# All heads' k first, and the triangular inverse from 32x32 blocks for all heads at once, in a decoder layer on one Trainium2 core

## Chip, cores and metric

One core of one Trainium2 chip. The metric is the device time of one launch in microseconds (us), the median of several runs. Everything is fp32. A projection multiplies in three passes of reduced fp32 (fp32r): weights and activations are each split into a high and a low part, and high by high, high by low and low by high are summed.

## What is computed

One layer (DEPTH is 1) on 512 tokens of 1024 channels, with two token mixers, a gated feed-forward part and a gated input embedding. The change touches the second mixer, the gated delta rule: 8 heads, key and value width 128, chunks of 64 tokens, so 64 chunks in all heads together. The kernel works on pairs of chunks, tiles of 128 tokens, four to a head.

```python
h = rmsnorm(x, attn_norm); proj = h @ w_in          # 1024 x 9232
qa, ka, va, qb, kb, vb, zb, bb, ab, gl = split(proj)
oa = diff_attention(rmsnorm(qa), rmsnorm(ka), va, lam, rel_bias)
qb, kb, vb = split(silu(causal_dwconv(cat(qb, kb, vb), conv_b)))
# gated_delta_rule, for each head and chunk of 64:
kkT = (k * beta) @ k.T
A = eye(64) + where(strict, kkT * decay, 0)
sol = triangular_solve(A, cat(v * beta, k * beta * exp(g)))
for chunk in chunks:                                 # carries state
    v_new = u - w @ state
    o = (q * exp(g)) @ state + (tril(q @ k.T) * decay) @ v_new
    state = state * exp(g_last) + k_dec.T @ v_new
mixed = gate0 * (oa @ w_br_a) + gate1 * (ob @ w_br_b); x = x + mixed @ w_out
# feed-forward (w_up, conv, silu gate, w_down) and embedding gate follow
```

## The kernel before, in words

The kernel is written by hand, engine by engine, with semaphores; the order on each engine is the order of the code. Weights come in chunks of 1024 x 128. For each chunk the DMA queue of SyncE (SP) loads it into one of four slots (`load`), GpSimd (in the profile POOL) makes its high part (L447) and low part (L432), and TensorE (PE) multiplies it with the normed activations (`gemm`, L493): eight steps of three matmuls of 512 columns. GpSimd takes a chunk when the chunk four before is multiplied.

`Fill.step(n)` runs the next n steps of the projection queue. TensorE's order is thus a weave: small matmuls of the attention and of the delta rule, with steps of projections between them, so that the other engines can answer in the meantime. How many steps stand where is in the tables `STEPS`, `STEPS_LEAD`, `STEPS_LATE` and `STEPS_LAST`, one for each kind of turn.

A turn (`turn`, one on each engine) takes head h's delta rule and head h + 1's attention together, and projects qb, kb, vb of head h + 1, zb of head h, and qa, ka, va of head h + 2: seven chunks, 56 steps. The first turn (`delta=False`) has attention only, the last only the delta rule. In a turn:

- Attention, for each of four blocks of queries: `scores` on TensorE (L598), `maxima` on VectorE (in the profile DVE; L1359, L1364), `softmax` on ScalarE (ACT; L960), `combine` on VectorE (L1374 to L1376), `turn_w` on TensorE (L605), `keep_w` on ScalarE; then `attend`.
- Short convolution: a first tap on ScalarE, three on VectorE (`conv`, L1390, L1394), then the silu by three ScalarE functions and a product on VectorE (`finish_silu`, L1405).
- The inverse of the unit triangular matrix of each chunk, by doubling: an inverse of blocks of size m gives that of size 2m. Six levels (n = 1 to 6), each with `ct` made by VectorE (`make_ct`, L1418), a group of matmuls (L674), a ScalarE copy (L1073), a second group (L686), a subtraction (L1488) and a 32x32-wise transpose (L1491) on VectorE. A group is eight matmuls of 64x64, two of them for each tile of 128 tokens, in the two halves of the array; in the last level four (L676, L688). For these the products k k^T (L644) are made at the start of the turn, and multiplied by the decay (L1459 to L1461), whose rows come from DRAM (`rows_of`) and are made by L1425. The norm of k enters as a scaling (`k_norm`, `start_x`, `start_wide`).
- The scan over the four tiles: `v_mm`, `vnew`, `kv`, `state` back and forth between TensorE and VectorE.

After the last turn come the gates and branches (`mix`), the output projection, the feed-forward part and the last gate. They are not touched.

## Time and profile before

| | us |
|---|---|
| median of 3 runs | 1222.64 |
| the runs | 1222.53 to 1222.65 |
| span of the profiled execution, first to last instruction | 1220.9 |
| TensorE busy | 1195.5 |
| VectorE busy | 682.4 |
| ScalarE busy | 538.4 |
| GpSimd busy | 617.8 |

No time is recorded for the profiled execution beside its span; the span is 1.7 us under the median. Busy time is the time in which an engine has an instruction under way; matmuls overlap, and the end of one is modelled, so the distance from start to start tells more than a duration. "Idle before" is the time in which the engine had nothing, in front of the instruction named, with what released it. An fp32 matmul leaves two records.

### The profile page before, as it was taken

What the parts mean: (1) busy time and instruction counts of PE and PEld (TensorE: products, weight loads), DVE (VectorE), ACT (ScalarE), POOL (GpSimd) and SP (SyncE); (2) the same over time, 40 slices, a digit from 0 to 9 for tenths busy, and PEclk for the clock granted to TensorE, in tenths of its full rate; (3) what the DMA queues carried; (4) which work ended last, traced back from release to release, by engine and by line L of the source; (5) the groups of instructions that cost most, each with busy time, mean ns of one, the idle gap of its engine ahead of it and who ended that gap; (6) DMA issues with size and microseconds to landing.
All of it is one profiled execution on the core that took longest, in us unless ns stands there. A gap on an engine that the chain in (4) does not pass through costs nothing.

```text
span 1220.9 us, 19031 instructions
## 1 busy us (share of the span) xinstructions
PE 1195.5 (98%) x6526; PEld 931.7 (76%) x6526; DVE 682.4 (56%) x1157; ACT 538.4 (44%) x923; POOL 617.8 (51%) x766
## 2 busy tenths in 40 slices
PE   6999999999999999999999999999999999999998
PEld 4766777777776777776777888888888888888886
DVE  5267576767768576767221323456677713651634
ACT  4364645455454636454232222354444423432542
POOL 5553443544453432635545645456656664573552
PEclk9999999999999999999999999999999999999999
DMA  8313130313121211312222342233333342232223
GB/s 261 91 43 99 27 93 18 99 33 95 35 78 53 62 35 43 106 52 69 70 70 77 105 163 86 87 99 107 98 93 103 89 118 85 87 111 78 71 80 90
DMA packets 192404, 102.66 MB, mean 84 GB/s; under 512 B 3798, under 2 KB 191177, under 8 KB 192329
## 3 DMA queue, kind: packets, MB, share of 16 engines
q1 hardware_dynamic: 191948, 101.55, 29.3%
q8 instruction: 42, 0.69, 0.2%
q14 instruction: 33, 0.27, 0.1%
q10 hardware_dynamic: 381, 0.15, 0.0%
HBM read 99.57 MB, written 2.13 MB: 83 GB/s over the span
## 4 chain that ended last, share of the span: by engine, by line
PE 90%; DVE 6%; ACT 3%; issue 1%; DMA 1%; ACTq 0%; DVEq 0%
PE bank L493 74%; PE bank L686 2%; PE bank L674 2%; PE bank L598 2%; PE bank L612 1%; PE bank L568 1%; DVE dec L1425 1%; PE bank L605 1%; DVE oa_lo L1585 1%; PE bank L644 1%; PE bank L723 1%; PE bank L627 1%; PE bank L653 1%; PE bank L731 1%; DMA slope<-bias_line 0%
## 5 line engine op out<-in xcount | busy, mean ns | idle before, releaser
L432 POOL TENSOR_TENSOR w_lo<-w_raw,w_hi 128x256 fp32r<-128x256 f32 x692 | 544.4, 819 | 261.2 <-ACT w_hi L877 255.5
L493 PE MATMUL bank<-hn_hi,w_hi 128*128 128x512 f32 x1000 | 423.8, 424 | 1.0 <-DVE o_a L1592 1.0
L493 PE MATMUL bank<-hn_hi,w_lo 128*128 128x512 f32 x1000 | 391.6, 392 | 0.0
L493 PE MATMUL bank<-hn_lo,w_hi 128*128 128x512 f32 x1000 | 391.2, 391 | 0.0
L447 POOL CAST w_hi<-w_raw 128x1024 fp32r<-128x1024 f32 x70 | 73.7, 1052 | 325.4 <-PE bank L493 296.9
L493 PEld LDWEIGHTS bank<-hn_hi,w_hi 128*128 128x128 f32 x1000 | 188.3, 188 | 48.6 <-issue 11.6
L493 PEld LDWEIGHTS bank<-hn_hi,w_lo 128*128 128x128 f32 x1000 | 187.8, 188 | 41.1
L493 PEld LDWEIGHTS bank<-hn_lo,w_hi 128*128 128x128 f32 x1000 | 188.6, 189 | 36.5 <-issue 6.5
L877 ACT ACTIVATE w_hi<-w_raw 128x1024 fp32r<-128x1024 f32 x111 | 117.9, 1062 | 75.8 <-PE bank L493 68.2
L1692 DVE SCALAR_TENSOR_TENSOR u<-vr,pt,u 128x511 f32<-128x511 f32 x88 | 88.8, 1009 | 8.0 <-DVE u L1692 0.2
L1686 DVE TENSOR_TENSOR vr<-bank,rs 128x512 f32<-128x512 f32 x44 | 30.4, 692 | 73.3 <-PE bank L493 67.8
L493 PE MATMUL bank<-fa_hi,w_hi 128*128 128x512 f32 x176 | 68.5, 389 | 0.0
L493 PE MATMUL bank<-fa_hi,w_lo 128*128 128x512 f32 x176 | 68.5, 389 | 0.0
L493 PE MATMUL bank<-fa_lo,w_hi 128*128 128x512 f32 x176 | 68.5, 389 | 0.0
L1211 ACT ACTIVATE u<-vr,pt 128x512 f32<-128x512 f32 x44 | 35.9, 816 | 38.9 <-DVEq L1687 38.2
L1073 ACT ACTIVATE ui<-bank 128x256 f32<-128x256 f32 (+1 forms) x48 | 18.4, 383 | 64.9 <-PE bank L674 58.7
L966 ACT ACTIVATE wT<-bank 128x128 f32<-128x128 f32 (+3 forms) x32 | 14.0, 438 | 72.0 <-PE bank L605 72.0
L1726 DVE TENSOR_TENSOR x<-x,bank 128x512 f32 x16 | 11.0, 688 | 61.3 <-PE bank L493 60.6
L1216 ACT ACTIVATE fa_hi<-tn 128x512 fp32r<-128x512 f32 x22 | 13.9, 633 | 65.6 <-DVE tn L1704 65.6
L960 ACT ACTIVATE pr<-bank,ast 128x128 f32<-128x128 f32 (+3 forms) x64 | 33.8, 528 | 18.7 <-DVE ast L1364 16.8
L1629 DVE TENSOR_TENSOR sg<-sg,bank 128x512 f32<-128x512 f32 x8 | 5.5, 688 | 62.9 <-PE bank L493 62.9
L1488 DVE TENSOR_TENSOR xi<-xi,bank 128x256 f32<-128x256 f32 x40 | 16.9, 421 | 41.9 <-PE bank L686 40.7
(277 smaller groups left out, 1770.4 us busy)
## 6 DMA issues: line engine op xcount, KB each, us to landing
w_raw<-in_w_in SPq DMA_DIRECT2D x73, 512.0 KB, 5.0
w_raw<-in_w_up SPq DMA_DIRECT2D x44, 512.0 KB, 3.8
w_raw<-in_w_down SPq DMA_DIRECT2D x16, 512.0 KB, 4.2
w_raw<-in_w_br_a SPq DMA_DIRECT2D x8, 512.0 KB, 4.2
w_raw<-in_w_br_b SPq DMA_DIRECT2D x8, 512.0 KB, 4.2
w_raw<-in_w_out SPq DMA_DIRECT2D x8, 512.0 KB, 4.2
w_raw<-in_w_ple_gate SPq DMA_DIRECT2D x8, 512.0 KB, 4.2
w_raw<-in_w_down SPq DMA_DIRECT2D x8, 384.0 KB, 3.5
```

Source lines behind the costliest of these rows:

```text
L432: ins = pool.tensor_tensor(wlo[c.slot][:, ks, :], raw[c.slot][:, ks, :], whi[c.slot][:, ks, :].bitcast(F32), ALU.subtract)
L447: pool.tensor_copy(whi[c.slot][:, :, :], raw[c.slot][:, :, :]).then_inc(high_ready, 1)
L493: mm = pe.matmul(acc, w[c.slot][:, i, :], xx[:, x0 + i, :], start=(i == 0 and n == 0), stop=last)
L598: mm = pe.matmul(bank[3 + j][:, 0:(i + 1) * P], qa[s, i * P:(i + 1) * P], ka[s, 0:(i + 1) * P], start=True, stop=True)
L674: mm = pe.matmul(packed(7, 0, t, q), ct[n % 2][q, t, :], xi[q, t, :], start=True, stop=True)
L686: mm = pe.matmul(packed(5, 0, t, q), xt[q, t, :], ui[q, t, :], start=True, stop=True)
L877: done(nc.scalar.activation(whi[c.slot][:, :, :], raw[c.slot][:, :, :], ACT.Copy), high_ready, c.number + 1)
L960: done(nc.scalar.activation(pr[j][:, 0:w], bank[3 + j][:, 0:w], ACT.Exp, bias=ast[:, 2 + j:3 + j], scale=-1.0, accum_out=ast[:, 4 + j:5 + j]),
L1073: done(nc.scalar.activation(ui[q, :, :], packed(7, part=q), ACT.Copy), "ui", h * (NL - 1) + n)
L1211: done(nc.scalar.activation(u[:, :], v[:, :], ACT.Identity, bias=col(PA_FBIAS + q * KF, f), scale=col(PA_TAP[2] + q * KF, f)), "u_made", 2 ...
L1686: done(V.tensor_tensor(v[:, :], bank[c.bank][:, :], rs[:, :], ALU.mult), bank_free[c.bank], c.uses + 1)
L1692: link(V.scalar_tensor_tensor(out=u[:, back:], in0=v[:, 0:T - back], scalar=col(PA_TAP[j] + q * KF, f), in1=u[:, back:], op0=ALU.mult, op1 ...
```

## The change

- The k projections of all eight heads are multiplied first (`stream.keys`), with their convolution, silu, products k k^T (`key_products`) and decay (`key_decay`, `lower`). The turns have six chunks, 48 steps; the first has five and a function of its own, `lead_turn`. k stays in `o_b`, whose place is free until each head's result is written.
- The level loop goes. `gather` transposes the four diagonal strips of 32 rows, so that each of the 128 partitions holds one 32x32 block: 32 tiles of 128 tokens, four blocks each. `substitute` then solves all 128 blocks at once by forward substitution, 31 steps of a product and a subtraction on VectorE over (31 - j)(j + 1) columns. It is cut into seven pieces that stand between head 0's attention pieces. `scatter` transposes the result into `xf`, which now lies in the free part of `o_a` for all heads and is zeroed by GpSimd at the start.
- The last two levels, 32 to 64 and the pair term that the second chunk of a tile needs, are made for all heads in `pair_low`, `pair_high` (32 matmuls of 32x32 each, two groups of each) and `half_low`, `half_high` (eight matmuls of 64x64 each, four groups of each), with ScalarE copies between them and VectorE taking the result (`pair_take`, `half_take`).
- The norms of k are read from the diagonal of the k products in one piece (`key_norms`).
- New step tables, and on ScalarE and VectorE another order inside the turn: the q silu comes before block 2's softmax, vb's silu before block 3's weights are kept.

```diff
--- before.py
+++ after.py
...
-LEVELS = (1, 2, 4, 8, 16, 32, 64)
-NL = len(LEVELS)
-STEPS = ((3, 2, 1, 1, 2), (2,) * 6, (1, 1, 1, 1, 1, 1), (3, (1, 1), (1, 1, 1), (1, 1, 1), (1, 1, 1)), (3, 6))
-STEPS_LEAD = (4, (5, 1, 1, 1, 2), (2, 1, 3, 2, 2, 2), (2, 0, 2, 0, 2, 0), (2, (1, 1), (1, 1), (1, 1), (1, 1)), (0, 1))
-STEPS_LATE = ((3, 2, 1, 1, 2), (2,) * 6, (1, 1, 1, 1, 1, 1), (3, (1, 0), (1, 1, 1), (1, 1, 1), (1, 1, 1)), (0, 0))
-STEPS_LAST = ((7, 2, 2, 3, 3), (3,) * 6, (4, 3, 3, 3, 3, 3), (3, (1, 1), (1, 1, 2), (1, 2, 2), (1, 2, 2)), (0, 0))
+SUB = 32
+ROWS = 4 * H
+STEPS = ((2, 3, 2, 3, 3, 1, 3, 3, 1, 5), ((1, 1), (1, 1, 1), (1, 1, 1), (1, 1, 1)), (3, 3))
+STEPS_LATE = ((3, 3, 1, 3, 3, 1, 2, 2, 1, 3), ((1, 0), (1, 1, 1), (1, 1, 1), (1, 1, 1)), (0, 0))
+STEPS_LAST = ((2, 3, 2, 3, 4, 1, 3, 3, 1, 3), ((1, 1), (2, 2, 2), (2, 2, 2), (2, 2, 2)), (0, 0))
...
+FIRST = ("qa", "ka", "va")
+TURN = ("qb", "vb", "zb", "qa", "ka", "va")
+LEAD = ("qb", "vb", "qa", "ka", "va")
+LATE = ("qb", "vb", "zb", "zl")
+KEY_BANKS = (5, 6, 7)
...
+            key_rows(0)
+            key_rows(1)
+            for n in range(5, H):
+                load(stream.keys.at(n), w_in0, COLS["kb"] + n * P)
+                key_rows(n - 3)
+            for n, name in enumerate(FIRST):
+                load(stream.first.at(n), w_in0, COLS[name])
+                key_rows(n + 5)
+            for n, name in enumerate(LEAD):
+                load(stream.lead.at(n), w_in0, COLS[name] + (AHEAD[name] - 1) * P)
+                if n == 0:
+                    rows_of(0)
...
+            f = Fill(*[gemm(stream.keys.at(n), hn_hi, hn_lo) for n in range(H)],
+                     *[gemm(stream.first.at(n), hn_hi, hn_lo) for n in range(len(FIRST))])
+            f.step(2)
...
+            def key_products(h):
+                b = KEY_BANKS[h % 3]
+                pe.wait_ge(sem("k_silu"), h + 1)
+                if h == 0:
+                    pe.wait_ge(sem("cum_turned"), 1)
+                elif h < 3:
+                    pe.wait_ge(sem("bias_ready"), H // 2)
+                else:
+                    pe.wait_ge(sem("lower"), h - 2)
+                for t in range(NT):
+                    s = slice(t * P, (t + 1) * P)
+                    mm = pe.matmul(tiles(b)[:, t, :], key(h)[:, s], key(h)[:, s], start=True, stop=True)
+                mm.then_inc(sem("kk"), 1)
...
+            for h in range(H):
+                f.step(2)
+                key_products(h)
+                f.step(6)
...
+            def pair_low(g):
+                b = (5, 7)[g]
+                pe.wait_ge(sem("blocks"), 1)
+                for n in range(HALF):
+                    m = g * HALF + n
+                    at = slice(n * SUB, (n + 1) * SUB)
+                    pe.matmul(bank[b][strip(1), at], dd[strip(0), m, SUB:2 * SUB], xf[strip(0), m, HEAD:HEAD + SUB],
+                              start=True, stop=True)
+                    mm = pe.matmul(bank[b][strip(3), at], dd[strip(2), m, SUB:2 * SUB], xf[strip(2), m, 3 * SUB:P],
+                                   start=True, stop=True)
+                mm.then_inc(sem("inverse_u"), 1)
...
+            def half_low(g):
+                b = (5, 7)[g % 2]
+                pe.wait_ge(sem("pairs"), 1 if g == 0 else 2)
+                if g > 1:
+                    pe.wait_ge(sem("xf_ready"), g - 1)
+                for n in range(8):
+                    m = g * 8 + n
+                    mm = pe.matmul(bank[b][UP, n * HEAD:(n + 1) * HEAD], lt6[LOW, m, :], xf[LOW, m, UP],
+                                   start=True, stop=True)
+                mm.then_inc(sem("inverse_u"), 1)
...
+            def lead_turn(at, fill):
+                f = Fill(*fill)
+                scores(0, 0)
+                f.step(8)
+                turn_w(0, 0)
+                f.step(2)
+                scores(0, 1)
+                f.step(8)
+                turn_w(0, 1)
+                f.step(2)
+                scores(0, 2)
+                f.step(6)
+                turn_w(0, 2)
+                f.step(2)
+                scores(0, 3)
+                f.step(4)
+                k_turn(0)
+                pair_low(0)
+                pair_low(1)
+                f.step(2)
+                turn_w(0, 3)
+                v_turn(0)
+                pair_high(0)
+                pair_high(1)
+                f.step(2)
+                attend(0)
+                half_low(0)
+                qk_sum(1, 0, at("qa"))
+                half_low(1)
+                f.step(1)
+                attention_sum(0)
+                half_high(0)
+                half_high(1)
+                f.step(1)
+                half_low(2)
+                qk_sum(1, 1, at("ka"))
+                half_low(3)
+                f.step(1)
+                half_high(2)
+                half_high(3)
+                f.rest()
...
-                for n in range(1, NL):
-                    if delta:
-                        if n < NL - 1:
-                            pe.wait_ge(sem("ct"), h * (NL - 1) + (n + 1))
-                        pe.wait_ge(sem("xi"), h * (NL - 1) + n)
-                        for t in range(NT):
-                            if n < NL - 1:
-                                for q in (LOW, UP):
-                                    mm = pe.matmul(packed(7, 0, t, q), ct[n % 2][q, t, :], xi[q, t, :], start=True, stop=True)
-                            else:
-                                mm = pe.matmul(packed(7, 0, t, UP), lt6[:, t, :], xi[LOW, t, :], start=True, stop=True)
-                        mm.then_inc(sem("level_u"), 1)
-                    f.step(first[n - 1])
-                    if delta:
-                        pe.wait_ge(sem("ui"), h * (NL - 1) + n)
-                        pe.wait_ge(sem("xt"), h * NL + n)
-                        if n == 1 and h > 0:
-                            pe.wait_ge(sem("ob_sum_read"), h)
-                        for t in range(NT if n < NL - 1 else 0):
-                            for q in (LOW, UP):
-                                mm = pe.matmul(packed(5, 0, t, q), xt[q, t, :], ui[q, t, :], start=True, stop=True)
-                        for t in range(NT if n == NL - 1 else 0):
-                            mm = pe.matmul(packed(5, 1, t, LOW), ui[UP, t, :], xt[UP, t, :], start=True, stop=True)
-                        mm.then_inc(sem("level_vt"), 1)
...
+                f.step(before[6])
+                if attention:
+                    k_turn(a)
+                f.step(before[7])
+                if attention:
+                    turn_w(a, 2)
+                f.step(before[8])
+                if attention:
+                    scores(a, 3)
+                pe.wait_ge(sem("xf_ready"), H // 2)
+                pe.wait_ge(sem("turned_read"), h + 1)
+                pe.matmul(tiles(7)[:, 0, :], xf[:, h * NT, :], vbt[:, 0, :], start=True, stop=True).then_inc(sem("v_mm"), 1)
+                f.step(before[9])
...
+            def lower(h):
+                b, d, m = KEY_BANKS[h % 3], decs[h % 2], slice(h * NT, (h + 1) * NT)
+                dve.wait_ge(sem("kk"), h + 1)
+                dve.wait_ge(sem("key_dec"), h + 1)
+                V.tensor_tensor(lt6[LOW, m, :], tiles(b)[LOW, :, UP], d[LOW, :, UP], ALU.mult)
+                V.tensor_tensor(dd[LOW, m, :], tiles(b)[LOW, :, LOW], d[LOW, :, LOW], ALU.mult)
+                done(V.tensor_tensor(dd[UP, m, :], tiles(b)[UP, :, UP], d[UP, :, UP], ALU.mult), "lower", h + 1)
...
+            def gather():
+                for b in range(4):
+                    at = SUB * (b % 2)
+                    ins = V.transpose(li[strip(b), :, :], dd[strip(b), :, at:at + SUB].rearrange("p n i -> p i n"))
+                link(ins)
+                done(V.transpose(ksum[:, :], wide(li)[:, 0:SUB * SUB:SUB + 1]), "k_sums", 1)
+                link(V.memset(xs[:, :, :], 0.0))
...
+            def substitute(j0, j1):
+                for j in range(j0, j1):
+                    n, w = SUB - 1 - j, j + 1
+                    part = prod[:, 0:n * w].rearrange("p (i c) -> p i c", c=w)
+                    link(V.tensor_tensor(part, li[:, w:SUB, j:w].to_broadcast([P, n, w]),
+                                         xs[:, j:w, 0:w].to_broadcast([P, n, w]), ALU.mult))
+                    link(V.tensor_tensor(xs[:, w:SUB, 0:w], xs[:, w:SUB, 0:w], part, ALU.subtract))
...
+            def scatter():
+                dve.wait_ge(sem("xf_zero"), 1)
+                place_rows(0, HEAD)
+                place_rows(2, 3 * SUB)
+                place_columns(1)
+                done(place_columns(3), "blocks", 1)
...
+            def lead_turn(at):
+                substitute(0, 6)
+                prep(0, 0)
+                prep(0, 1)
+                substitute(6, 11)
+                maxima(0, 0)
+                substitute(11, 15)
+                combine(0, 0)
+                steps(conv(0, 0, at("qb")))
+                maxima(0, 1)
+                substitute(15, 20)
+                combine(0, 1)
+                steps(finish_silu(0, 0))
+                substitute(20, 23)
+                maxima(0, 2)
+                substitute(23, 26)
+                steps(conv(0, 2, at("vb")))
+                combine(0, 2)
+                substitute(26, 31)
+                maxima(0, 3)
+                scatter()
+                combine(0, 3)
+                scatter_rest()
...
+            for h in range(H):
+                steps(conv(h, 1, stream.keys.at(h)))
+                if h == 0:
+                    for n in range(H // 2):
+                        bias_copy(n)
+                if h > 1:
+                    lower(h - 2)
+                if h > 0:
+                    key_decay(h - 1)
+                steps(finish_silu(h, 1))
+            lower(H - 2)
+            key_decay(H - 1)
+            lower(H - 1)
+            gather()
+            scale_rows()
...
```

TensorE, in a turn of before, from the scores of block 2 on: one level group (L674), two steps, the second group (L686). The names after the arrow are the inputs, the numbers the output's size.

```order
L598 MATMUL bank<-ka,qa 128x384 x2
L674 MATMUL bank<-xi,ct 64x64 x8
L493 MATMUL bank<-hn_hi,w_hi 128x512
L493 MATMUL bank<-hn_lo,w_hi 128x512
L493 MATMUL bank<-hn_hi,w_lo 128x512
...
L686 MATMUL bank<-ui,xt 64x64 x8
```

Twelve such groups stood in each turn, each in front of its steps.

TensorE now, in `lead_turn`, after a step of projection (L524): k's transposes (L676 in the new file), then the 32x32 groups (L696, L698; 64 such rows for both `pair_low`).

```order
L524 MATMUL bank<-hn_lo,w_hi 128x512
L524 MATMUL bank<-hn_hi,w_lo 128x512
L676 MATMUL bank<-sq,o_b 128x128 x4
L696 MATMUL bank<-o_a,dd 32x32
L698 MATMUL bank<-o_a,dd 32x32
```

The level groups have left the turns, and all heads' small matmuls follow each other here without steps between them.
VectorE, in a turn of before: level operations between the attention's and the convolution's.

```order
L1418 TENSOR_TENSOR ct<-lt,sq 128x256
L1488 TENSOR_TENSOR xi<-xi,bank 128x256
L1491 STREAM_TRANSPOSE xt<-xi 128x256
L1390 SCALAR_TENSOR_TENSOR kb<-bank,pt,kb 128x511
L1390 SCALAR_TENSOR_TENSOR kb<-bank,pt,kb 128x510
L1394 SCALAR_TENSOR_TENSOR kb<-bank,pt,kb 128x509
L1359 TENSOR_TENSOR bank<-bank,bias 128x256 x2
L1364 TENSOR_REDUCE ast<-bank 128x1 x2
L1488 TENSOR_TENSOR xi<-xi,bank 128x256
```

These level operations leave VectorE's turns.

VectorE now, ahead of head 0's attention: gather, the norms, the row scaling and the first steps of the substitution (L1637, L1639; 62 such rows, up to 256 columns).

```order
L1618 STREAM_TRANSPOSE li<-dd 32x1024 x4
L1620 STREAM_TRANSPOSE ksum<-li 128x32
L1621 MEMSET xs 128x1024
L1626 TENSOR_TENSOR kz<-kz,gates 128x32
L1628 STREAM_TRANSPOSE kzb<-kz 128x32
L1629 COPY xs<-kzb 128x32
L1630 TENSOR_TENSOR li<-li,kzb 128x1024
L1637 TENSOR_TENSOR prod<-li,xs 128x31
L1639 TENSOR_TENSOR xs<-xs,prod 128x31
L1637 TENSOR_TENSOR prod<-li,xs 128x60
L1639 TENSOR_TENSOR xs<-xs,prod 128x30x2
```

They stand in front of everything of the lead; `prep(0, 0)`, for which TensorE's `scores(0, 0)` waits, follows six of the steps.
TensorE, in a turn of before, the last rows between the scores of block 3 and its turned weights (L605); ahead of these rows stand seven more steps and three level groups.

```order
L493 MATMUL bank<-hn_hi,w_lo 128x512
L688 MATMUL bank<-xt,ui 64x64 x4
L493 MATMUL bank<-hn_hi,w_hi 128x512
L493 MATMUL bank<-hn_lo,w_hi 128x512
L493 MATMUL bank<-hn_hi,w_lo 128x512
L622 MATMUL bank<-sq,kb 128x128 x4
L708 MATMUL bank<-vbt,xf 128x128
...
L493 MATMUL bank<-hn_hi,w_lo 128x512
L605 MATMUL bank<-sq,pr 128x128 x4
L586 MATMUL bank<-sq,va_raw 128x128 x4
```

The two level groups, and more of them further up, stood between scores and weights.

TensorE now, from those scores (L650 here) to the turned weights (L657): one small matmul (L829) and five steps, of which the middle is left out.

```order
L650 MATMUL bank<-ka,qa 128x512 x2
L829 MATMUL bank<-vbt,o_a 128x128
L524 MATMUL bank<-hn_hi,w_hi 128x512
L524 MATMUL bank<-hn_lo,w_hi 128x512
L524 MATMUL bank<-hn_hi,w_lo 128x512
...
L524 MATMUL bank<-hn_hi,w_lo 128x512
L657 MATMUL bank<-sq,pr 128x128 x4
L638 MATMUL bank<-sq,va_raw 128x128 x4
```

Of what stood between the two, k's transposes and the level groups are gone, the first to an earlier place.

## Rows read from the trace of the kernel before

**Rows 1.** The page's first lines: span, and one engine's busy time, share and instructions.

```profile
span 1220.9 us, 19031 instructions
PE 1195.5 (98%) x6526; PEld 931.7 (76%) x6526; DVE 682.4 (56%) x1157; ACT 538.4 (44%) x923; POOL 617.8 (51%) x766
```

**Rows 2.** Busy us in stretches: PE, weight load, VectorE, ScalarE, GpSimd, then granted clock, DMA.

```profile
51.00:97.00 46.00, 42.42 (x184) 29.62 (x182) 29.19 (x56) 27.65 (x61) 22.82 (x27) 1.00 0.35 91
163.00:229.00 66.00, 65.40 (x445) 47.75 (x444) 46.84 (x93) 34.70 (x75) 28.25 (x36) 1.00 0.22 58
```

**Rows 3.** TensorE by line, shapes apart, one of the level loop's groups: busy us, mean ns, idle before.

```profile
L674 PE MATMUL bank<-xi,ct 64*64 64x64 f32 x640 | 27.2, 224 | 0.0
```

**Rows 4.** TensorE in order of time, one level group between projection matmuls.

```profile
238.58 0.39 PE L493 MATMUL bank<-hn_hi,w_lo 128*128 128x512 f32 x1
238.90 0.68 PE L674 MATMUL bank<-xi,ct 64*64 64x64 f32 x16
239.51 0.50 PE L493 MATMUL bank<-hn_hi,w_hi 128*128 128x512 f32 x1
...
240.08 0.40 PE L493 MATMUL bank<-hn_hi,w_lo 128*128 128x512 f32 x1
```

**Rows 5.** VectorE's groups by line, shapes apart.

```profile
L1418 DVE TENSOR_TENSOR ct<-lt,sq 128x256 f32<-128x256 f32 x40 | 24.4, 610 | 2.2 <-DVE qb L1394 1.1
L1425 DVE SCALAR_TENSOR_TENSOR dec<-crow,gates,sq 128x128 f32<-128x128 f32 x32 | 14.5, 515 | 0.4 <-DVE vb L1394 0.2
L1390 DVE SCALAR_TENSOR_TENSOR kb<-bank,pt,kb 128x511 f32<-128x511 f32 x8 | 6.0, 750 | 0.3
L1491 DVE STREAM_TRANSPOSE xt<-xi 128x256 f32<-128x256 f32 x32 | 14.3, 445 | 1.1
L1493 DVE STREAM_TRANSPOSE xt<-xi 32x128 f32<-32x128 f32 x8 | 2.4, 300 | 0.3
```

**Rows 6.** VectorE in order of time: two runs of one operation, and a small one.

```profile
92.85 0.17 DVE L1433 TENSOR_TENSOR kz<-kz,gates 128x4 f32<-128x4 f32 x1
...
246.48 0.43 DVE L1418 TENSOR_TENSOR ct<-lt,sq 128x256 f32<-128x256 f32 x1 [0.16 <-DVE qb L1394]
250.56 0.84 DVE L1418 TENSOR_TENSOR ct<-lt,sq 128x256 f32<-128x256 f32 x1
```

**Rows 7.** All engines in order of time, from a block's scores to its turned weights.

```profile
73.17 1.13 PE L598 MATMUL bank<-ka,qa 64*128 64x512 f32 x4
...
74.44 0.77 DVE L1359 TENSOR_TENSOR bank<-bank,bias 128x256 f32<-128x256 f32 x2 [0.16 <-PE bank L598]
75.23 1.29 DVE L1364 TENSOR_REDUCE ast<-bank 128x1 f32<-128x512 f32 x2
...
77.42 0.69 ACT L960 ACTIVATE pr<-bank,ast 128x512 f32<-128x512 f32 x1
...
79.55 1.11 DVE L1376 SCALAR_TENSOR_TENSOR pr<-pr,ast 128x512 f32<-128x512 f32 x1
...
80.71 0.66 PE L605 MATMUL bank<-sq,pr 128*128 128x128 f32 x4 [0.27 <-DVE pr L1376]
```

**Rows 8.** TensorE in order of time, the same two places in a turn.

```profile
190.34 1.13 PE L598 MATMUL bank<-ka,qa 64*128 64x512 f32 x4
...
201.49 0.60 PE L605 MATMUL bank<-sq,pr 128*128 128x128 f32 x4
```

**Rows 9.** Order of time at the start, TensorE and then GpSimd.

```profile
8.80 3.19 PE L537 MATMUL bank<-sq,x_tok 128*128 128x128 f32 x12 [8.80 <-DVE x_tok L1290]
...
18.80 0.78 PE L493 MATMUL bank<-hn_hi,w_hi 128*128 128x512 f32 x1
19.37 0.58 PE L493 MATMUL bank<-hn_lo,w_hi 128*128 128x512 f32 x1
19.78 0.40 PE L493 MATMUL bank<-hn_hi,w_lo 128*128 128x512 f32 x1
...
12.69 1.04 POOL L447 CAST w_hi<-w_raw 128x1024 fp32r<-128x1024 f32 x1 [12.23 <-DMA w_raw<-in_w_in]
```

778 lines of the change are left out of this document (405 added, 373 removed).

## The prediction

> **What bounds the kernel now.** I read the shares of busy time first, then the stretches, then TensorE's groups and its order of time. TensorE is busy 98% of the span [rows 1]. In the stretches the reader is to see that this holds from head to head: in a turn of 66 us (the work from one `scores(a, 0)` to the next) TensorE lacks 0.6 us, VectorE is busy 47 and ScalarE 35; only between 51 and 97 us, where the first head has attention and no delta rule, are 3.6 us missing [rows 2]. So time goes only where TensorE's own work goes, and it comes back wherever TensorE must wait. The change takes work from TensorE and gives VectorE a long serial chain. The sum has therefore two parts: TensorE's work, and TensorE's waits.
>
> I sum against the profiled execution, whose span is 1220.9 us. The median of the runs is 1222.64, so 1.7 us lie around the span, and I add them at the end. A measurement of this kernel tells about 0.2%, 2.4 us, from no change.
>
> **TensorE's work, removed.** Per head there are six levels of two groups of small matmuls, 96 groups in all (the 640 records of [rows 3] are the first groups of five levels; each fp32 matmul leaves two). What one costs is read from the order of time, not from the 0.68 us that it is drawn with: projection matmuls follow each other by 0.23 us, but from the one that starts at 238.58 to the third after the group at 240.08 there are 1.50 us where three steps would take 0.69 [rows 4]. So a group costs 0.81 us, and 96 cost 77.8 us. The k projections (eight steps of 0.69 us each) and the k products move from the turns to the front; they are no saving.
>
> **TensorE's work, added.** Four groups of 32 matmuls with 32 columns (`pair_low`, `pair_high`), and eight groups of eight 64x64 matmuls on one half of the array (`half_low`, `half_high`). For the latter the nearest row is the level group itself, eight matmuls of 64x64 of which two halves run side by side: of its 0.81 us I take 0.43 as four in a row (0.107 each: 64 columns, four passes, at 2.4 GHz) and 0.38 as the change-over; eight in a row make 0.86 + 0.38 = 1.24 us, and eight groups 9.9 us. No row shows 32 columns. At the columns' pace (half of 0.107 a matmul, two strips side by side) a pair group takes 0.85 us; at the pace of L674's records (0.61 us for 16 [rows 4], 64 records here) 2.4. I take 1.7, in the middle; four make 6.8 (3.4 to 9.8). Together 16.7. So TensorE's work falls by 77.8 - 16.7 = **61.1 us**.
>
> The Trainium skill gives this one price directly: TensorEngine Tiling (Array Packing), "Instruction Overhead", says that a matmul of one column takes as long as one of 60. By it a 32-column matmul costs no less than a 64-column one, and the pair groups would stand near the upper end, 3 us more than I take. No run here shows it yet.
>
> **Waits in front.** From about 25 us TensorE runs the eight k projections, then qa, ka, va of head 0, with the k products two steps into the projection after next. Per head VectorE has there three taps (3 x 0.75), the decay rows (14.5 us for eight heads, 1.8 each), three products with the decay and the silu product (512 columns each in all, 1.3 and 0.75), near 6.2 us [rows 5]; TensorE has 5.5 and 0.95 for the k product. They balance; I count 1 us of waits, and 0.7 at the bias matmuls, whose copies now stand behind a convolution. After the last k silu VectorE alone carries the chain up to `blocks`, for which `pair_low` waits:
> - lower for two heads and one decay: 4.3
> - eight 32x32 transposes of 1024 columns, four to gather and four to scatter. 128 columns take 0.30 and 256 take 0.445 us [rows 5], so 1024 take about 1.3: 10.5 (lower bound as computed; if the far strides double it, 21)
> - the zeroing of xs, row scaling and three small ScalarE steps for the norms: 4.3
> - the substitution: 31 steps of two linked operations. The columns of a step are (31-j)(j+1), 5456 in the sum. 4 columns take 0.17 and 256 take 0.43 us when undisturbed, so 0.165 us + 1.04 ns a column, and 0.04 from link to link: 62 x 0.205 + 2 x 5456 x 0.00104 = 24.1. But the same 256 columns take 0.61 in the mean and 0.84 at worst, in TENSOR_TENSOR from SBUF, when GpSimd is at work [rows 5, 6]. I take 26, a quarter of the operations disturbed; the ends are 24 and 43
> - prep 1.6, head 0's maxima (6.5, by widths from the 0.77 + 1.29 of block 3 in [rows 7]), three combines (3.9), two convolutions and a silu (5.3): 17.3
> - tap and scores to wait for after each resumption of TensorE: 2.5.
>
> Sum 65 us. TensorE has over the same stretch 46 steps of 0.69, 31.7, and 7.5 of k product, scores, turns and sums: 39.2. So it waits **26 us**, in five pieces of 4 to 7 us before `scores(0, 0)`, three `turn_w` and `pair_low`. After `blocks` the rounds TensorE, ScalarE, VectorE of the two lower levels hide behind attend and the sums of squares, but for 1 us. The waits of before in this part go: 3.6 us by [rows 2] and 0.3 ahead of them. Net 1 + 0.7 + 26 + 1 - 3.9 = **+24.8 us**.
>
> **Waits in the turns.** A turn shrinks from 66 to 49.8 us of TensorE's work: eight steps (5.5), a k product (0.95) and twelve level groups (9.7) are gone. Those groups had been cover for the softmax. The chain from the scores of block 3 to its turned weights is, in an undisturbed place, VectorE from 74.44, ScalarE's two exponentials to 78.2, VectorE to 80.66, TensorE at 80.71; the scores ended at 74.3, so 6.1 to 6.4 us [rows 7]. In a turn of before, 10 us of other work lay between the two [rows 8]; the order now has one small matmul and five steps, 3.75 us. So TensorE must wait 2.4 us each turn. By the same rows block 2 has 5.8 us of chain (ScalarE takes the q silu ahead of the softmax) behind 4.75 us of cover, wait 1.0; and the sum of squares of ka, for which ScalarE must first finish qa's root, waits 0.7. With the chain's lower end that is 4.0 us in each of six turns, 24; the late turn has three steps and two steps fewer of cover there, 6.5; the last turn's wait for ob_scaled 1.2. VectorE and ScalarE themselves are not full, some 34 and 27 of 53 us. The 5 us of waits that the seven turns have now (0.6 each by [rows 2]) are replaced. Net **+26.7 us**.
>
> **Costed at nothing.** GpSimd's zeroing of xf, 4096 columns, 4 us by its CAST of 1024 in 1.05, is hidden ahead of its first cast, which waits for data until 12.69 us [rows 9]; uncovered it would be 4 us. The k loads stand in SP's queue behind `cum_turned` and behind the rows of the decay two heads back; each gets there 10 us or more before its multiplication. If the decays came late, the loads of qa, ka, va would be next. GpSimd splits seven projections in 28 us of a turn now [rows 2], so six take 24 of 50.
>
> **Sum.** 1220.9 - 61.1 + 24.8 + 26.7 = 1211.3; with the 1.7 us around it **1213 us**, 0.8% faster. In place: head 0's delta turn starts near 183 us instead of 97, and from there on everything is 96 us shorter.
>
> **Rivals.**
> 1. *The covers suffice* (chance 0.2). I chain single durations; if waits overlap more than I see, the turns lose 10 instead of 32 us and the front 20. Then 1213 - 22 - 6 = 1185; half of it gives 1199. For it: the order keeps five steps in reserve at each turn's end. Against it: [rows 7].
> 2. *VectorE's chain in front is longer, and the change loses* (0.17). Place: substitution, gather, scatter; mechanism: contention with GpSimd, which splits weights meanwhile, and strides of 128 or 256 bytes in the transposes. At their upper ends they add 15 and 10 us, each in full to TensorE's wait: 1213 + 25 = 1238; from 7 us on it is no gain beyond the measurement, from 12 us on a loss. Half of it gives about 1226, and I price it at 1231. For it: 0.84 against 0.43. Against it: GpSimd itself runs dry while TensorE waits.
> 3. *TensorE's clock falls in the waits* (0.1). At its start, after 8.8 us without work, it works 10 us on transposes, and then the first projection matmuls are still 0.57 and 0.41 apart, and 0.23 later [rows 4, 9]; the page's granted clock reads full (2.4 GHz) in this stretch all the same, so only the spacing tells. If each of five waits brings this back for as much work as there, 5 us each, of which the later waits hide the half: +13, 1226. The waits of under 1 us in the turns [rows 2] did no such thing; 4 to 7 us are not shown. The Trainium skill, TensorE: Matmul & The Clock Gate, "HAM oscillation", warns of just this: idle gaps send the clock to 1.2 GHz and each burst starts cold. By it this rival would be the rule and not the exception; the small waits of this trace neither bear it out nor refute it.
> 4. *The levels were no cost*, because other work took their place (0.03): 1240 or more. The order of time in rows 4 speaks against it.
>
> **How the numbers follow.** My forecast has 0.5, at 1213, with its own range of 1204 to 1222. The range of 1195 to 1231 leaves out the far halves of rivals 1 and 2. Faster by over 0.2% (under 1220.2): nearly nine tenths of the forecast, all of rival 1 and a fifth of rival 2 and 3 together: 0.69. Within 0.2%: 0.12. Slower: most of rival 2, rival 4 and some of 3: 0.19.
>
> **What would show it.** TensorE's busy time near 1134 us, and its idle time before `scores(0, 0)`, the `turn_w` of head 0 and the first 32x32 group in pieces of 4 to 7 us; turns of 53 to 54 us, with waits of 2 to 3 us before the four transposes of `turn_w(a, 3)`, put down to VectorE's pr; the substitution's operations at 0.2 to 0.45 us. Head 0's delta turn starts near 183 us. I am wrong if a turn takes under 51 or over 56 us, if the substitution takes over 35 us, or if projection matmuls after a wait follow by more than 0.23 us for long.

## The result, and the profile after

| | before | changed |
|---|---|---|
| median, us | 1222.59 | 1240.51 |
| the runs, us | 1222.46 to 1222.65 | 1238.85 to 1241.61 |
| span of the profiled execution, us | 1220.9 | 1239.8 (own time 1241.6) |
| TensorE busy, us | 1195.5 | 1153.6 |

The change makes the kernel slower by 1.4%: ratio 1.0144, 95% interval 1.013 to 1.0159, against 1213 forecast and outside its range. Against the 1211.3 us forecast for the span of the profiled execution, 28.5 us are missing.

The page's first lines, its clock row and its shares of the chain, to be read beside [rows 1]:

```profile
span 1239.8 us, 16629 instructions
PE 1153.6 (93%) x5502; PEld 909.3 (73%) x5502; DVE 662.9 (53%) x1061; ACT 509.2 (41%) x798; POOL 620.3 (50%) x767
PEclk9997879999999999999999999999999999999999
PE 75%; DVE 16%; ACT 5%; issue 3%; ACTq 0%; DVEq 0%
```

TensorE's busy time fell by 41.9 us where 61.1 were forecast, and its idle time rose from 25.4 to 86.2 us, by 60.8 where 51.5 were forecast. The clock row has a dent that the one before did not have. The stretches (the columns of [rows 2]) say where; the first five are the lead, the work from the last k to head 0's delta turn, then come two full turns:

```profile
97.00:113.00 16.00, 3.98 (x17) 2.68 (x17) 15.03 (x24) 2.70 (x6) 10.73 (x14) 0.70 0.37 98
113.00:137.00 24.00, 17.34 (x63) 12.66 (x61) 20.81 (x44) 5.01 (x13) 8.28 (x10) 0.85 0.00 1
137.00:151.00 14.00, 8.53 (x30) 5.83 (x30) 12.05 (x24) 4.34 (x10) 3.96 (x5) 0.88 0.00 0
151.00:166.00 15.00, 7.88 (x29) 5.33 (x29) 12.70 (x19) 3.44 (x8) 0.00 (x0) 0.73 0.00 1
166.00:196.00 30.00, 29.11 (x430) 22.73 (x430) 19.46 (x25) 14.73 (x24) 4.64 (x6) 0.85 0.37 90
252.00:308.00 56.00, 51.34 (x244) 37.27 (x242) 31.49 (x61) 27.24 (x53) 25.20 (x30) 1.00 0.24 62
308.00:365.00 57.00, 52.38 (x243) 38.32 (x242) 31.48 (x61) 27.24 (x53) 25.19 (x30) 0.97 0.23 61
```

The mean granted clock of the lead is 0.70 to 0.88 of full speed: it goes to and fro between its two levels, 2.4 and 1.2 GHz. Of the two turns the second lasts 1.6 us longer, at 0.97. TensorE in order of time shows its waits in the lead and in one turn (from the block-0 scores at 308.00 to the next at 364.92):

```profile
112.67 0.80 PE L650 MATMUL bank<-ka,qa 64*128 64x128 f32 x4 [12.02 <-DVE ka L1515]
123.71 0.47 PE L657 MATMUL bank<-sq,pr 128*128 128x128 f32 x1 [2.92 <-DVE pr L1542]
137.20 0.56 PE L657 MATMUL bank<-sq,pr 128*128 128x128 f32 x2 [3.94 <-DVE pr L1542]
151.19 0.90 PE L657 MATMUL bank<-sq,pr 128*128 128x128 f32 x3 [5.46 <-DVE pr L1542]
166.26 0.26 PE L696 MATMUL bank<-o_a,dd 32*32 32x32 f32 x1 [7.20 <-DVE o_a L1646]
...
321.40 0.44 PE L657 MATMUL bank<-sq,pr 128*128 128x128 f32 x2 [0.57 <-DVE pr L1542]
329.26 0.55 PE L657 MATMUL bank<-sq,pr 128*128 128x128 f32 x3 [1.08 <-DVE pr L1542]
337.70 0.66 PE L657 MATMUL bank<-sq,pr 128*128 128x128 f32 x4 [2.26 <-DVE pr L1542]
338.19 0.60 PE L638 MATMUL bank<-sq,va_raw 128*128 128x128 f32 x4
338.55 0.58 PE L524 MATMUL bank<-hn_hi,w_hi 128*128 128x512 f32 x1
338.93 0.63 PE L524 MATMUL bank<-hn_lo,w_hi 128*128 128x512 f32 x1
339.36 0.63 PE L524 MATMUL bank<-hn_hi,w_lo 128*128 128x512 f32 x1
...
360.41 1.13 PE L625 MATMUL bank<-sqr,sq 128*128 128x512 f32 x2 [0.71 <-ACT sqr L1043]
```

The five waits of the lead are there, 31.5 us in all (26 forecast), at the places named, though of 2.9 to 12.0 us and not of 4 to 7; the turns' waits too, 4.6 us a turn (4.0 forecast), the one before block 1's `turn_w` not foreseen. And behind the wait of 2.26 us the projection matmuls are 0.43 us apart, not 0.23: the slow clock. VectorE's groups in the lead, shapes apart, answer to [rows 5]:

```profile
L1618 DVE STREAM_TRANSPOSE li<-dd 32x1024 f32<-32x1024 f32 x4 | 8.0, 2002 | 0.1
L1646 DVE STREAM_TRANSPOSE o_a<-xs 32x1024 f32<-32x1024 f32 x4 | 7.7, 1927 | 0.1
L1642 DVE STREAM_TRANSPOSE o_a<-xs 32x1024 f32<-32x1024 f32 x3 | 6.6, 2191 | 0.1
```

A transpose of 1024 columns takes 2.0 us, not 1.3. From the last k silu (88.1) to `blocks` (166.2) VectorE's chain takes 78.1 us where I had 65, and VectorE is without work for 6.2 of them.

From these rows two theories. **Theory 1:** the clock is what is missing; it makes TensorE's work in the lead longer, and the 13 us by which head 0's delta turn is late (196.1 instead of 183) are the clock's. **Theory 2:** VectorE's chain sets the end of the lead at any clock, and the turns lack cover; the clock costs only where TensorE itself is the bound. The runs that follow were judged against the kernel before on the same chip (1222.4 to 1222.8 us); differences below are to the 1240.5 of the changed kernel, whose runs spread by about 1.4 us each way.

### The profile page after: what moved, and what is told of

Its sections match the earlier page's. It is cut to its first block, busy times and chain, and to the rows that moved or that the text cites. A ratio compares the mean times of both kernels' runs of the same rounds, so it can differ in the third digit from the quotient of the medians.

```text
span 1239.8 us, 16629 instructions
## 1 busy us (share of the span) xinstructions
PE 1153.6 (93%) x5502; PEld 909.3 (73%) x5502; DVE 662.9 (53%) x1061; ACT 509.2 (41%) x798; POOL 620.3 (50%) x767
## 4 chain that ended last, share of the span: by engine, by line
PE 75%; DVE 16%; ACT 5%; issue 3%; ACTq 0%; DVEq 0%
PE bank L524 64%; DVE pr L1542 2%; PE bank L664 1%; DVE pr L1541 1%; PE bank L625 1%; ACT pr L1077 1%; DVE dec L1587 1%; DVE o_b L1556 1%; DVE qb L1556 1%; DVE xs L1639 1%; PE bank L650 1%; DVE vb L1556 1%; DVE prod L1637 1%; PE bank L657 1%; DVE ast L1530 1%
## 5 line engine op out<-in xcount | busy, mean ns | idle before, releaser
L524 PE MATMUL bank<-hn_hi,w_hi 128*128 128x512 f32 x1000 | 421.7, 422 | 1.0 <-DVE o_a L1815 1.0
L524 PE MATMUL bank<-hn_hi,w_lo 128*128 128x512 f32 x1000 | 395.4, 395 | 0.0
L524 PE MATMUL bank<-hn_lo,w_hi 128*128 128x512 f32 x1000 | 394.9, 395 | 0.0
L524 PEld LDWEIGHTS bank<-hn_hi,w_hi 128*128 128x128 f32 x1000 | 191.0, 191 | 49.0 <-issue 15.2
L524 PEld LDWEIGHTS bank<-hn_hi,w_lo 128*128 128x128 f32 x1000 | 190.7, 191 | 42.1
L524 PEld LDWEIGHTS bank<-hn_lo,w_hi 128*128 128x128 f32 x1000 | 191.3, 191 | 38.2 <-issue 5.7
L524 PE MATMUL bank<-fa_hi,w_hi 128*128 128x512 f32 x176 | 68.5, 389 | 0.0
L524 PE MATMUL bank<-fa_lo,w_hi 128*128 128x512 f32 x176 | 68.5, 389 | 0.0
L524 PE MATMUL bank<-fa_hi,w_lo 128*128 128x512 f32 x176 | 68.5, 389 | 0.0
L657 PE MATMUL bank<-sq,pr 128*128 128x128 f32 x80 | 16.8, 312 | 42.2 <-DVE pr L1542 42.2
L657 PEld LDWEIGHTS bank<-sq,pr 128*128 128x128 f32 x80 | 9.4, 150 | 54.2 <-DVE pr L1542 53.9
L650 PE MATMUL bank<-ka,qa 64*128 64x128 f32 (+3 forms) x128 | 27.4, 506 | 12.8 <-DVE ka L1515 12.8
```

Source lines behind the costliest of these rows:

```text
L524: mm = pe.matmul(acc, w[c.slot][:, i, :], xx[:, x0 + i, :], start=(i == 0 and n == 0), stop=last)
L650: mm = pe.matmul(bank[3 + j][:, 0:(i + 1) * P], qa[s, i * P:(i + 1) * P], ka[s, 0:(i + 1) * P], start=True, stop=True)
L657: mm = pe.transpose(bank[3][:, t * P:(t + 1) * P], pr[0][:, t * P:(t + 1) * P], ident)
```

## Experiments

**The clock alone, in the lead.**

```diff
+W = (48, 18, 22, 28, 34)
...
+            def warm(n):
+
+                for _ in range(n):
+                    pe.matmul(bank[5][:, :], hn_hi[:, 0, 0:P], hn_hi[:, 0, :], start=True, stop=True)
...
+                pe.wait_ge(sem("lower"), H)
+                warm(W[0])
                 scores(0, 0)
                 f.step(8)
+                warm(W[1])
                 turn_w(0, 0)
...
```

> The changed kernel, with 150 single-pass matmuls of 512 columns into a free bank placed in the five waits before scores(0, 0), turn_w(0, 0) to turn_w(0, 2) and pair_low (48, 18, 22, 28, 34 of them, 0.23 us each at full clock); they compute nothing that is used and fit into the waits. Theory 1 (the clock did it: TensorE's busy time is 1153.6 us where 1134 was forecast, and the clock is the whole reason why head 0's delta turn starts 13 us late): the granted clock stays at 2.4 GHz from 97 to 196 us, scores(1, 0) start near 183 instead of 196.1, and the time falls by 13 us to about 1227. Theory 2 (VectorE's chain up to `blocks` sets the end of the lead, at whatever clock TensorE runs): the clock is full too, but pair_low starts at 162 to 165 instead of 166.3, only the 3 to 4 us in which VectorE waited for slow TensorE work and the 4 us of slow work behind 166 come back: 1232 to 1236. If the slow clock cost nothing: 1240.

Measured: 1234.2 us (1233.5 to 1236.1), 6.3 less. Two stretches of the lead, and TensorE at the start of head 0's delta turn:

```profile
97.00:113.00 16.00, 14.93 (x66) 11.62 (x65) 14.94 (x27) 2.70 (x6) 10.08 (x12) 1.00 0.31 84
151.00:166.00 15.00, 15.00 (x102) 11.38 (x102) 13.51 (x19) 3.00 (x7) 0.00 (x0) 1.00 0.00 1
```

```profile
191.77 0.49 PE L651 MATMUL bank<-ka,qa 64*128 64x128 f32 x4 [0.74 <-DVE ka L1527]
```

In the lead the clock was full but for one short piece near 125 us (0.93 between 113 and 137), behind the one longer wait that was left, of 1.9 us. Yet `pair_low` started at 165.4, only 0.8 earlier than without: up to there VectorE's chain sets the pace. From there to `scores(1, 0)` it took 26.3 us instead of 29.9, so the clock costs about 4 us in the lead (0.8 and 3.5), not 13. Theory 2. (The rest of the 6.3 came with two slow pieces of the late turn that this run happened not to have.)

**The chain without the substitution, and the longest wait moved.**

```diff
             def substitute(j0, j1):
 
-                for j in range(j0, j1):
+                for j in ():
```

> The 31 steps of the substitution are left out, so what follows computes with inverse blocks that hold the diagonal alone. They take 28.7 us of VectorE from start to start. Theory 2 (VectorE's chain): nearly all of it comes out of TensorE's waits before pair_low (31.5 us in all), the remaining waits are near 5 us, the clock's drops in the lead go with them: 25 to 33 us less, 1207 to 1215. Theory 1 (the clock alone is what is missing, VectorE's chain is covered by something else): 13 us less at most, 1227.

```diff
-                substitute(0, 6)
-                prep(0, 0)
-                prep(0, 1)
-                substitute(6, 11)
+                substitute(0, 11)
                 maxima(0, 0)
...
             gather()
+            prep(0, 0)
+            prep(0, 1)
             scale_rows()
```

> Only VectorE's order changes: the two operations that make qa and ka of head 0 stand behind the gather and not behind the first six steps of the substitution. The longest single wait of TensorE, 12.0 us before scores(0, 0), must shrink to about 4. Theory 2 (what counts is the length of VectorE's chain up to `blocks`, and it is the same): the later waits grow by as much, pair_low starts at 162 to 166 us, and only part of VectorE's 6 us of idle time between its pieces and of the slow clock goes: 1236 to 1240. Rival (the wait before scores(0, 0) is itself the loss): 8 us less, 1232.

Without the substitution 1218.7 us, 21.8 less; the first 32x32 group started at 146.9 instead of 166.3. That is beyond theory 1 (13 at most), and short of the 25 to 33 I expected: between 113 and 137 us VectorE was then busy for 12.9 us only. Attention's own round between the three engines had probably become the chain; no run tests that by itself. With the order changed 1239.9 us, 0.7 less, within the spread: `scores(0, 0)` at 106.3 instead of 112.7, but 8.4 us of wait before the next `turn_w` instead of 2.9, and `pair_low` at 165.4. A single wait is not a loss by itself; the chain's length is.

**Why a transpose takes 2.0 us.**

```diff
-                place_rows(0, HEAD)
-                place_rows(2, 3 * SUB)
-                place_columns(1)
-                done(place_columns(3), "blocks", 1)
+                for b in range(4):
+                    ins = V.transpose(xf[strip(b), 8 * b:8 * b + 8, :], xs[strip(b), :, :])
+                done(ins, "blocks", 1)
```

> The four 32x32 transposes before `blocks` (2.05 us each) are given contiguous operands of the same size, so their blocks land in wrong places of xf. If strides are what makes 1024 columns cost 2.0 us, each takes 1.3 to 1.4 us (a 512-column one of o_a takes 0.70) and the time falls by 2.6 us to 1238. If it is the size, or GpSimd, they stay at 2.0 and the time at 1240.5.

Measured: 1235.7 us, 4.8 less (2.6 expected), more than the 3.3 us of the transposes. They took 1.24 us each; the gather, left with its stride of 256 bytes, 2.0 as before:

```profile
L1618 DVE STREAM_TRANSPOSE li<-dd 32x1024 f32<-32x1024 f32 x4 | 8.0, 2011 | 0.1
L1652 DVE STREAM_TRANSPOSE o_a<-xs 32x1024 f32<-32x1024 f32 x4 | 4.9, 1236 | 0.1
```

So it is the stride, and it costs 0.8 us per 1024 columns. The Trainium skill, SBUF — State Buffer, has a note on "SBUF cachelines": accesses in a row that each go to another 16-byte line pay a penalty. The trace agrees in direction; the size, 60%, is this run's. Of the 1.5 us that the transposes don't account for, 0.9 are there already when the gather begins (93.7 instead of 94.7), before anything that the edit touches: they are the spread from run to run.

**Cover in the turns.**

```diff
-STEPS = ((2, 3, 2, 3, 3, 1, 3, 3, 1, 5), ((1, 1), (1, 1, 1), (1, 1, 1), (1, 1, 1)), (3, 3))
+STEPS = ((2, 3, 2, 3, 4, 1, 3, 4, 1, 8), ((1, 0), (1, 1, 1), (1, 1, 1), (1, 1, 1)), (0, 3))
```

> Only the table of fill steps of the six full turns changes: block 3's softmax gets 8 steps of cover instead of 5, blocks 1 and 2 one step more each, taken from the three steps before the sum of squares of qa, from one behind t = 0 of the scan and from the reserve at the turn's end. If too little cover makes the waits (0.57 + 1.08 + 2.27 + 0.70 = 4.6 us a turn): the first three go to 0 to 0.3 each, the last grows to at most 2, turns take 52 to 53 us instead of 55.3, and the turns in which the clock dropped (56.6 and 56.9) take no more than the others: 1217 to 1224. If the waits only move (to the scan, to the sums or to scores(a, 0)): turns stay at 55 and the time is 1236 to 1241.

Measured: 1215.7 us (1214.4 to 1216.8), 24.8 less, and 0.6% under the kernel before (ratio 0.9942, 0.9928 to 0.9955). Turns are 52.44 us apart (the first 51.8). One of them:

```profile
320.47 0.55 PE L657 MATMUL bank<-sq,pr 128*128 128x128 f32 x3 [0.54 <-DVE pr L1542]
329.22 0.66 PE L657 MATMUL bank<-sq,pr 128*128 128x128 f32 x4 [0.56 <-DVE pr L1542]
347.71 1.13 PE L625 MATMUL bank<-sqr,sq 128*128 128x512 f32 x2 [0.72 <-ACT sqr L1043]
```

That is a little beyond the 1217 expected at best. Nothing moved elsewhere: the wait for the sum of squares stayed at 0.7, none appeared in the scan. No turn had the slow clock. The six turns won 22.4 us, of which 4.6 by the clock (the run below).

**The clock alone, in the turns.**

`idle(n)` issues the same matmuls as `warm(n)` above; the late turn is the one with `more_a` false.

```diff
                 if attention:
+                    if not more_a:
+                        pe.wait_ge(sem("ob_sum_read"), h)
+                        idle(8)
                     turn_w(a, 2)
...
                 if attention:
+                    if h > 0:
+                        pe.wait_ge(sem("ob_sum_read"), h)
+                    idle(8 if more_a else 10)
                     turn_w(a, 3)
```

> The changed kernel with idle matmuls only in the waits of the turns: 8 before each turn_w(a, 3) (1.8 of 2.27 us), in the late turn 8 and 10 before turn_w(7, 2) and turn_w(7, 3). The waits' ends and the order are as they were. If the slow clock in turns (turns 0, 2 and 5 took 56.6 to 56.9 us, the others 55.3; two drops in the late turn) comes from these waits: all six turns take 55.3 to 55.5 us and the time falls by 6 to 8 us: 1232 to 1235. If the drops come from elsewhere in a turn: three turns of 56.9 remain, 1240.

Measured: 1233.6 us (1232.7 to 1234.4), 6.9 less. All turns take 55.4 us (the first 55.0), the stretch of the six has full clock, and so has what follows:

```profile
196.00:528.00 332.00, 314.64 (x1491) 230.60 (x1489) 187.97 (x365) 161.81 (x316) 150.72 (x181) 1.00 0.24 63
```

The drops do come from these waits. In the changed kernel a wait of 2.1 to 2.3 us, the only longer one in a turn, brought the slow clock in three turns of six, at 1.6 us each; no drop in the turns of any run stands behind one of the waits of 0.5 to 1.1 us. In between lies one of 1.9 us in the lead, behind which the clock fell in e1 and not in e13 below.

**What a level group had cost.**

```diff
+                    self.f, self.h, self.left = f, h, 12 if h < H - 2 else 0
...
+                        self.f.step()
+                        if self.left:
+                            self.left -= 1
+                            for t in range(NT):
+                                for q in (LOW, UP):
+                                    pe.matmul(bank[7][q, t * HEAD:(t + 1) * HEAD], key(self.h)[q, 0:HEAD],
+                                              key(self.h)[q, t * P:t * P + HEAD], start=True, stop=True)
```

> The changed kernel with twelve groups of eight 64x64 matmuls put back into each of the six full turns, on idle data into a free bank, one behind each of the first twelve fill steps (the work that the change took out, without its waits). At 0.81 us a group, as forecast, a turn takes 55.3 - 0.6 + 9.7 = 64.4 us; at 0.68, the time a group is drawn with, 62.9. Whichever it is, 12 groups a turn must cost more than the 8.9 us that turns actually lost of TensorE's work, if the last level's two groups of four matmuls were cheaper than the rest: 64.4 says so, 63.6 says that all groups cost 0.74. The waits before turn_w(a, 2) and turn_w(a, 3) remain.

Measured: 1288.8 us, and 64.87 us a turn. Of these 3.4 are waits (0.42, 2.27 and 0.70; block 1's is covered) and 1.6 the clock, which fell in every turn. So the work is 59.9 us, 9.2 more than the changed kernel's 50.7: 0.77 a group. Alone between steps a group costs 0.81 as in [rows 4], right ahead of other small matmuls 0.61:

```profile
323.45 0.40 PE L524 MATMUL bank<-hn_hi,w_lo 128*128 128x512 f32 x1
323.78 0.68 PE L793 MATMUL bank<-o_b 64*64 64x64 f32 x16
...
324.96 0.40 PE L524 MATMUL bank<-hn_hi,w_lo 128*128 128x512 f32 x1
325.28 0.68 PE L793 MATMUL bank<-o_b 64*64 64x64 f32 x16
325.89 1.16 PE L815 MATMUL bank<-qb,o_b 128*128 128x128 f32 x8
```

A turn of the kernel before took 66.6 us (228.46 to 295.09) with 0.6 of waits; less eight steps, a k product and the 50.7 that remain, its twelve groups were worth 8.9 us, not my 9.7. What I expected of this run, that the last level's two groups of four matmuls had been the cheaper ones, the trace of the kernel before refutes:

```profile
328.07 0.39 PE L493 MATMUL bank<-hn_hi,w_lo 128*128 128x512 f32 x1
328.39 0.68 PE L676 MATMUL bank<-xi,lt 64*64 64x64 f32 x8
...
329.58 0.40 PE L493 MATMUL bank<-hn_hi,w_lo 128*128 128x512 f32 x1
```

From the matmul before the group to the third behind it are 1.51 us, as the 1.50 of [rows 4]: four matmuls on one half of the array cost the same 0.81 as eight on two halves side by side. What was cheaper are the groups next to other small matmuls, three of twelve in a turn of before and four of twelve here. With these at 0.61 the twelve come to 9.1 and 8.9 us (9 x 0.81 + 3 x 0.61, 8 x 0.81 + 4 x 0.61), within 0.3 of what was measured, 8.9 and 9.2.

**A shorter gather, which first made it slower.** ScalarE lays out the diagonal blocks of each head (`compact(h)`), so that one transpose of 128 partitions replaces four.

```diff
+                for b in range(4):
+                    at = SUB * (b % 2)
+                    ins = nc.scalar.activation(xs[strip(b), :, m], dd[strip(b), m, at:at + SUB].rearrange("p n i -> p i n"), ACT.Copy)
+                done(ins, "compacted", h + 1)
...
                 if h > 0:
                     key_decay_exp(h - 1)
+                if h > 1:
+                    compact(h - 2)
...
-                for b in range(4):
-                    at = SUB * (b % 2)
-                    ins = V.transpose(li[strip(b), :, :], dd[strip(b), :, at:at + SUB].rearrange("p n i -> p i n"))
-                link(ins)
+                dve.wait_ge(sem("compacted"), H)
+                link(V.transpose(li[:, :, :], xs[:, :, :]))
```

> The gather as one transpose of 128 partitions with contiguous operands: ScalarE copies the diagonal blocks of each head, as lower makes them, into a tile that is laid out for it (four copies of 128 columns a head, in the phase of the keys where it is half idle). Chain before: four transposes, 8.05 us. Now 1.3 us for one (1.24 us was the contiguous one of the run e3_flat_tr), and some 1.2 us for the last head's copies. Theory 2: 5 to 6 us come out of the chain and of the time: 1234 to 1236. If a transpose over 128 partitions costs four times one over 32, or ScalarE's copies hold up the silus of the keys: no gain, 1240 or more.

> The steps of e4_steps, the gather of e6_compact, and qa and ka of head 0 behind three steps of the substitution instead of six. If the effects add: 1215.7 less 5 to 7, 1209 to 1211. If the shorter chain is eaten by more time at half clock: 1213 or more.

> The same with idle matmuls in the five waits of the lead (8, 14, 18, 24, 24 of them, 0.23 us each). e1_warm_lead won 6.3 us, of which some 4 in the lead and 2 in the late turns. If the clock's price stands beside the chain: 4 to 6 us under e7_steps_compact, 1203 to 1207. If the two overlap (a shorter chain has shorter waits, in which the clock falls less): 2 us or less.

Measured: 1255.3, 1233.1 and 1229.3 us. None of the three gains came; the first is 19 us over its forecast and the other two 22. (Of the three only the first had named the way it went, ScalarE's copies holding up the silus.) The transpose did take 1.25 us for 128 partitions. But in the key phase k products stood 10.1 to 10.9 us apart instead of 6.4 from the fourth head on. ScalarE in order of time, then VectorE in two rounds:

```profile
72.70 0.63 ACT L1183 ACTIVATE dec<-dec 128x512 f32<-128x512 f32 x1 [2.70 <-DVE dec L1600]
73.36 1.71 ACT L1151 ACTIVATE xs<-dd 32x128 f32<-32x128 f32 x4
75.10 0.69 ACT L1100 ACTIVATE o_b<-bank,pt 128x512 f32<-128x512 f32 x1
78.35 0.63 ACT L1116 ACTIVATE silu<-o_b 128x512 f32<-128x512 f32 x1 [2.56 <-DVEq L1575]
...
61.02 1.14 DVE L1600 SCALAR_TENSOR_TENSOR dec<-crow,gates,sq 128x128 f32<-128x128 f32 x4
69.26 3.35 DVE L1600 SCALAR_TENSOR_TENSOR dec<-crow,gates,sq 128x128 f32<-128x128 f32 x4
72.64 1.10 DVE L1585 TENSOR_TENSOR o_b<-o_b,silu 128x512 f32<-128x512 f32 x1
```

ScalarE was half idle, and yet on the critical path: ScalarE and VectorE wait for each other in a ring (tap, convolution, silu, product, decay, exponential), and the copies stood in it. By themselves they made the one round in which the decay still took 1.1 us 1.4 us longer (7.8). From the next on, the decay took 3.0 to 3.3 us and the silu product 1.1 instead of 0.7: the longer rounds had brought GpSimd's splitting of the weights beside them (from 69.2 to 73.2 here; in the changed kernel it falls mostly beside other work). That is the other 2.5 us of a round of 10.3. The next run puts the copies where ScalarE waits for the convolution:

```diff
                 first_tap(h, 1, stream.keys.at(h))
+                if h > 2:
+                    compact(h - 3)
```

> As e6_compact, but ScalarE makes the copies of a head behind the first tap of the head three later, while it would wait for VectorE's convolution (2.56 us), and not on the way from one silu to the next tap. In e6_compact a head of the key phase took 10.3 us instead of 6.4, the transpose itself 1.25 instead of 8.05. If the four copies (1.76 us) in the cycle of ScalarE and VectorE made that loss: heads are back at 6.4 to 6.7 us, the chain up to `blocks` is 5 us shorter, 1234 to 1237. If it was the writes into the strided tile or GpSimd: heads stay at 8 to 10 us and the time over 1245.

Measured: 1238.5 us, 2.0 less than the changed kernel, short of the 1234 to 1237 expected. The heads are back at 6.4 us (one at 7.9), the gather ends at 99.4 instead of 102.7, but qa and ka of head 0 are made from 111.2 on, as before (111.1). The gain was lost in between:

```profile
104.86 0.67 DVE L1651 TENSOR_TENSOR xs<-xs,prod 128x31 f32<-128x31 f32 x1
105.57 0.95 DVE L1649 TENSOR_TENSOR prod<-li,xs 128x60 f32<-128x60 f32 x1
```

while GpSimd split weights (from 100.5 to 109.3 with hardly a pause). Held back until ka is made:

```diff
-            for c in [stream.first.at(n) for n in range(len(FIRST))] + [stream.lead.at(n) for n in range(len(LEAD))]:
+            for c in [stream.first.at(n) for n in range(len(FIRST))] + [stream.lead.at(0)]:
+                both(c)
+            pool.wait_ge(sem("qka_ready"), 3)
+            for c in [stream.lead.at(n) for n in range(1, len(LEAD))]:
                 both(c)
```

> e9_compact_hidden with GpSimd held: it splits the second and later weights of the lead only after ka of head 0 is made. In e9_compact_hidden the first eight operations of the substitution (31 to 112 columns) take 0.6 to 0.95 us while GpSimd splits weights, 5.3 us from 104.2 to 109.5; in the changed kernel all but the first two of the same run alone at 0.22 to 0.28. If GpSimd beside it is what slows VectorE's TENSOR_TENSOR: these eight take 2.3 us, scores(0, 0) start 2.5 to 3 us earlier (at 109.5 to 110), the operations behind them (12 to 15 of the substitution) are slowed instead, and pair_low moves by 0 to -2 us: 1236 to 1239. If the slowness comes from the operations' small size or the tile's place: they stay at 0.6 to 0.95.

```profile
102.59 0.22 DVE L1652 TENSOR_TENSOR prod<-li,xs 128x60 f32<-128x60 f32 x1
102.85 0.22 DVE L1654 TENSOR_TENSOR xs<-xs,prod 128x60 f32<-128x60 f32 x1
...
112.94 3.30 POOL L460 TENSOR_TENSOR w_lo<-w_raw,w_hi 128x256 fp32r<-128x256 f32 x4
...
113.97 0.82 DVE L1652 TENSOR_TENSOR prod<-li,xs 128x231 f32<-128x231 f32 x1
114.83 0.82 DVE L1654 TENSOR_TENSOR xs<-xs,prod 128x231 f32<-128x231 f32 x1
```

The same operations, of 31 and 60 columns, take 0.21 to 0.22 us without GpSimd beside them and 0.59 to 0.95 with it; one of 231 columns takes 0.40 alone and 0.82 with it. In the trace of the changed kernel, of the 62 operations of the substitution ten are slowed so, by 5.4 us in all; all ten, and only one of the others, lie beside an instruction of GpSimd. `scores(0, 0)` started at 107.3, but the next seventeen operations were slowed instead, `pair_low` came at 168.4, and the time was 1240.7: nothing won. Transposes, and operations that read a PSUM bank, kept their times beside GpSimd. The Trainium skill, SBUF — State Buffer, says why under "SBUF: two separate sides": VectorE and GpSimd share a pair of ports, and an operation of VectorE with two inputs in SBUF waits for the whole instruction of a GpSimd that reads SBUF. The traces agree: a slowed operation of 31 to 112 columns is about as long as one of GpSimd's pieces, 0.7 us, and in the changed kernel the slow gather, which has one input, had been a good cover for GpSimd. One operation does not fit: the row scaling over 1024 columns, with two inputs too, took 1.2 us in both runs.

**Do the parts add?**

> The steps of e4_steps, the hidden copies of e9_compact_hidden with qa and ka three steps into the substitution, idle matmuls in the lead (8, 14, 18, 24, 24) and in the two long waits of the late turn (8, 10). If the effects add: 1215.7, less 5 for the gather, less 3 to 5 for the clock behind `blocks`, less 2 to 3 for the late turn: 1203 to 1206. If the clock's price and the chain overlap: 1207 to 1211.

> The steps of e4_steps and the idle matmuls of e1_warm_lead in the lead and of e10_warm_turns in the late turn; the gather as it is. If the price of too little cover (e4_steps, 24.8 us) and that of the clock in the lead and the late turn (4.4 and 2.9 us) add: 1208 to 1209. If they overlap: 1211 or more. Beside e12_combined (1212.7) it also says what the hidden copies are worth in the sum: by e9_compact_hidden 2 us at most.

> e12_combined with GpSimd held as in e14_hold and more idle matmuls where it still waited (30, 20, 18, 24, 28). e12_combined still has half clock for 6.8 us from 105.7 and from 163.7, and waits of 6.8 and 3.0 us. If these count: 1206 to 1209. If not: 1210 to 1213.

Measured: 1212.7 us (1208.7 to 1212.9) with the shorter gather (e12), 1211.5 (1210.9 to 1212.7) without it (e13), 1213.6 (1211.3 to 1214.8) with it and GpSimd held (e15). e13, the steps and the idle matmuls alone, has full clock; VectorE is busy for 80 of the 94 us of its lead, TensorE, idle matmuls included, for 89:

```profile
97.00:191.00 94.00, 89.34 (x713) 68.57 (x711) 80.47 (x133) 30.29 (x60) 27.20 (x33) 1.00 0.15 39
```

It came 2.5 to 3.5 us over its expectation: the clock was worth 4.2 us on top of the steps, not 7.3, since the run with the steps had only one slow piece left in its late turn, and the lead gave 3.9 as before. No gain of the gather is to be seen on top; but the runs with it had fewer idle matmuls and some slow clock left in the lead (0.990 and 0.994 over the span against 0.998), so its worth in the sum is not measured by itself. The best version by the median is e13, 0.9% under the kernel before (ratio 0.9912, interval 0.9898 to 0.9925); e12, at 0.9904 (0.989 to 0.9918), can't be told from it.

## Why the prediction was wrong, point by point

Measured on the profiled execution, the 28.5 us are: lead 13.1 (head 0's delta turn at 196.1, not 183), six turns 13.6 (336.4 us, not 6 x 53.8), the late turn and what follows 1.8. The steps of the sum that failed are the length of VectorE's chain in front, the size of the work removed, a wait left out in each turn, and TensorE's clock, which the sum held at full. Two of the prediction's own signs of being wrong showed: turns of 56.6 to 56.9 us, three of the six, and matmuls 0.43 us apart behind a wait.

- **TensorE's work, removed**: 77.8 us was too high. The 0.81 of a group between projection matmuls holds (e11: 0.81), for the last level's groups too, but three of the twelve in a turn stand next to other small matmuls and cost 0.61: 8.9 us a head by the turns' lengths. This step of the sum failed by 6 to 7 us, 5 of them in the six turns. It was to be seen in the order of time, of which I had read one place. (The "three steps" of 0.69 us in that reading are three matmuls, one step.)
- **TensorE's work, added**: forecast 16.7, some 3 us too high. At full clock (e1) two pair groups took 2.1 us, 1.07 each, near the lower bound of 0.85 and not 1.7; at the lower clock of the changed kernel 1.8. A half group took about 1.1 (1.24 forecast). That makes 12.6 us for the twelve groups from their starts to the next matmul's, and 13 to 14, an estimate, with the change-overs. The Trainium skill, TensorEngine Tiling (Array Packing), "Instruction Overhead", says that a matmul of one column takes as long as one of 60. The measurement speaks against the use I made of it: in e1 two fp32 matmuls of 32 columns side by side took 0.067 us, and one of 64 columns 0.117.
- **Waits in front**: places right, the sum of VectorE's chain 13.1 us short, so the step failed. The eight transposes took 16.3 us, not 10.5: I took contiguous rows for strided ones and kept the stride for the range's end. The substitution took 28.7 from start to start, not 26. The decay and the last products took 6.6, not 4.3: the last decay took 3.1 us beside GpSimd, where the one before it, without, took 1.1, and 0.9 went in a wait for ScalarE. VectorE waited for others another 5.0 us, not 2.5. So rival 2 came true in part, at about half its price. That the whole lead is late by just these 13.1 us is partly chance: behind `blocks` the clock cost 3.5 us, about what the added groups were forecast too dear.
- **Waits in the turns**: blocks 2 and 3 and the sum of squares were forecast at 1.0, 2.4 and 0.7, and are 1.1, 2.3 and 0.7. Block 1's 0.57 is missing: 3.4 us in six turns. The step was right in kind. (The waits of before that it subtracts are put at 5 us; seven turns at 0.6 make 4.2.) What I did not draw from it: the waits are a matter of one table, and the table was not fitted to turns that have lost twelve groups of cover. That alone is worth 24.8 us (e4, with the clock's share in it), more than the change's whole loss.
- **TensorE's clock** was the rival with 0.1 and should have been part of the forecast. It costs some 4 us in the lead, most of them behind `blocks` (e1), and 6.9 in the turns and the late turn (e10), 11 in all, near the 13 I gave it, but in other places: in the lead most of it is hidden behind VectorE, while turns with waits of 2.3 us, which I thought harmless, pay for it. My argument, that waits under 1 us had done no such thing, was about other waits. The Trainium skill, TensorE: Matmul & The Clock Gate, "HAM oscillation", tells of a kernel whose idle gaps send the clock to 1.2 GHz, so that each burst of work starts slow. The trace agrees, with a granted clock of 0.70 to 0.88 in the stretches of the lead; I weighed too lightly a rule that spoke against the change where the trace was silent.
- **The number and its chances**: four steps failed the same way, each towards longer; in the six turns these are 5 us of work removed, 3.4 of block 1's wait and 4.6 of the clock, 13.0 of the 13.6. Only the price of the added groups erred the other way. The range had room for one of the rivals, not for two and a mis-sized term at once.

The account by run: e4 24.8 us for cover (4.6 of it the clock), e1 some 4 for the clock in the lead, e3 3 to 5 for half of the strides. What stays open is what the shorter gather is worth once the clock is full, and why one operation with two inputs kept its time beside GpSimd.

## What to carry to other kernels

Work taken from a busy engine is also cover taken from its neighbours' chains: when a change shortens a turn, refit the interleaving before judging the change; here one line of numbers turned +1.4% into -0.6%. An engine that is half idle can still stand in a ring of waits, and most of what is added to it there is paid (e6: 1.4 of 1.8 us a round), and more if the new rhythm sets a third engine's work beside the ring. A wait of TensorE as long as the 2.3 us of these turns should be priced with the slow clock behind it, where TensorE is the bound, and not where another engine is.

## What the runs showed of the hardware

- The clock can fall after waits of 2.1 to 2.3 us that come once in a turn of 55 us, in three turns of six; matmuls of 512 columns are then 0.43 us apart instead of 0.23 for about 3 us. Idle matmuls in the wait kept it at 2.4 GHz in every turn (e10).
- A group of small fp32 matmuls between projection matmuls costs 0.81 us, whether eight of 64x64 on two halves of the array or four on one; next to other small matmuls 0.61.
- A VectorE transpose of 1024 columns takes 1.24 us with contiguous operands, over 32 partitions (e3) or over 128 (e9) alike, and 1.9 to 2.2 us with a stride of 128 to 512 bytes on one side or both.
- A VectorE operation on two SBUF tensors of 60 columns takes 0.22 us, and 0.77 to 0.95 while GpSimd works on tensors in SBUF (e14, e9).
- ScalarE takes 0.43 us for a copy of 128 columns on 32 partitions with strided output (e6).
